# Expert items of 32 slots instead of 64 in a routed streaming step, with four column tiles per product and 8 KB weight runs

## The chip, the cores and the metric

The kernel runs as one program on one core of a Trainium2 chip. The metric is the device time of one execution in microseconds (us); lower is better. The kernel before was executed three times for its time and once more under the hardware profiler, and the changed kernel is measured beside it. The program has five instruction streams: TensorE (PE in the profile; its weight loads are PEld), VectorE (DVE), ScalarE (ACT), GpSimd (POOL) and SyncE (SP), which issues the large transfers.

## The reference, cut to what matters

```python
# N = 384 tokens (256 of a prompt, 8 x 16 of running streams), D = 1024, float32
x = x + mixers(rms_norm(x)) @ w_o                      # first stage, not touched by the change
xn = rms_norm(x, norm2_g)                              # (384, 1024)
lg = xn @ rg_w + rg_b;  p = softmax(lg);  grp = argmax(p)          # 1 group of 4
le = (xn @ re_w + re_b) restricted to grp; the best two of its 8 experts, softmax of the two, times p[grp]
combine = per token two non-zero weights over the 32 experts
for e in range(32):                                    # D_EXPERT = 512
    hdn = silu(xn @ w_gate[e]) * (xn @ w_up[e])        # w_gate, w_up: (1024, 512) each
    out = out + combine[:, e:e+1] * (hdn @ w_down[e])  # w_down: (512, 1024)
y = rms_norm(x + out, final_norm_g)
```

Each of the 384 tokens goes to 2 of 32 experts, 768 pairs in all. For the inputs used, the reference's routing gives the experts 0 to 31 this many tokens: 34 41 7 14 | 8 9 13 6 | 18 20 7 5 | 21 3 7 13 | 32 73 35 37 | 6 12 17 18 | 10 48 18 62 | 28 72 5 69. The bars separate groups of four.

## The kernel before, in words

The first 380 us hold the mixers: 20 chunks of weights are loaded (SP), split into a high and a low part (ACT, POOL) and multiplied (line 1294); convolutions run on DVE. The change does not touch them. From about 403 us on the kernel works off **items**. An item is one expert with up to T = 64 of its tokens ("slots"); an expert with more tokens has more items, and every expert has at least one. There are 35 items. PE, ACT and DVE each run the same loop over them, written as a loop over 16 pairs of experts with the body of `side` 0 and of `side` 1 one after the other, and inside each side a loop over the expert's items. How many items an expert has, and the running numbers, are read from `table` by each engine at the head of each side (`value_load`, four of them on PE: lines 1471 to 1477). In side 1 the first item is written out by itself (line 1482) and the further ones stand in a second body behind a test `n > 1` (line 1483), so that the PE program of a pair holds three item bodies.

One item on PE (function `item`, lines 1427 to 1468) does in this order:

- gate and up (line 1420): the 64 slots as two halves of 32; for each half in use 8 row blocks times 4 column tiles of 128 x 256 weights in float32, results in one PSUM bank, 32 partitions per column tile. The second half runs only if its slots hold tokens (`second_slots`, read from the table);
- for a body that adds back (`c` is not None: side 0 always, side 1 from its second item on), `combine` (line 1413): the collected outputs of the items before, `y_hi` and `y_lo`, are multiplied by a 0/1 matrix `back_to` for three tiles of tokens, and DVE adds the three tiles to `x_tok` (line 1138, `add_rows`);
- gather of the next item's tokens (line 1382): 8 blocks times 3 bfloat16 parts times 3 token tiles, 72 products with the 0/1 matrix `pick`, which DVE builds (lines 1087 and 1091);
- transposes of the hidden rows (line 1452), then down (line 1463): 4 row blocks times 2 column tiles of 128 x 512 weights.

ACT computes silu (line 791), copies the transposed rows (794) and rounds the output to `y_hi` (800); DVE multiplies gate and up and the routing coefficient (1170), scales the gathered tokens (1101), builds `pick`, `back_to` (1181, 1184) and the coefficients (1144, 1149) and forms `y_lo` (1200). The output of an item goes to the half `side` of the partitions of `y_hi` and `y_lo`, so that two experts are collected before rows are added back.

The 192 MiB of expert weights pass through a ring of six slots of 2 MiB, three (gate, up, down) for each of two experts. SP fills them in 1 MiB transfers (line 442), in the order gate, up, gate, up, down, down of each expert; a transfer waits until the expert two before has finished with that half of the slot (`gate_up_half`, `gate_up_done`, `down_half`, `down_done`). The source rows of gate and up are runs of 2 KB, those of down 4 KB.

## Time and profile before

| | before |
|---|---|
| median of 3 runs | 950.26 us (949.14 to 950.53) |
| the profiled execution's own time | 950.75 us |
| its span, first to last instruction | 949.0 us |
| granted TensorE clock, mean over the span | 0.950 |
| PE busy | 834.0 us (88%) |
| DVE busy | 559.4 us (59%) |
| ACT busy | 303.2 us (32%) |
| POOL busy | 270.4 us (28%) |
| bytes moved by DMA | 250.00 MB |
| chain that ended last: PE, DMA | 67%, 20% of the span |

The span is the profiled execution from its first to its last instruction; 1.75 us of the execution's time lie around it. "Busy" counts an engine's instructions; for PE it also counts the time in which products wait in the pipeline, so that a busy PE need not be at its peak. An idle time is put down to what ended it; "issue" means that nothing the profile shows was waited for: the engine's own instruction stream was late.

### The profile page before, as it was taken

What the parts mean: (1) busy time and instruction counts of PE and PEld (TensorE: products, weight loads), DVE (VectorE), ACT (ScalarE), POOL (GpSimd) and SP (SyncE); (2) the same over time, 40 slices, a digit from 0 to 9 for tenths busy, and PEclk for the clock granted to TensorE, in tenths of its full rate; (3) what the DMA queues carried; (4) which work ended last, traced back from release to release, by engine and by line L of the source; (5) the groups of instructions that cost most, each with busy time, mean ns of one, the idle gap of its engine ahead of it and who ended that gap; (6) DMA issues with size and microseconds to landing.
All of it is one profiled execution on the core that took longest, in us unless ns stands there. A gap on an engine that the chain in (4) does not pass through costs nothing.

```text
span 949.0 us, 22550 instructions
## 1 busy us (share of the span) xinstructions
PE 834.0 (88%) x8411; PEld 622.4 (66%) x8412; DVE 559.4 (59%) x1516; ACT 303.2 (32%) x522; POOL 270.4 (28%) x136
## 2 busy tenths in 40 slices
PE   3999999979999999286999777887999988879994
PEld 2999999969999988153555444544565545445562
DVE  3066797899432342844677455545666764646766
ACT  4432875543358332511122111112112221211112
POOL 3745899875767780400000000000000000000000
PEclk9999999989999999598999799979999999999997
DMA  5744244344433323949899999999999999999901
GB/s 210 220 132 134 90 133 134 90 138 134 133 102 120 133 76 125 399 154 377 340 393 396 393 396 392 396 392 397 392 397 392 397 392 397 392 397 392 394 2 66
DMA packets 110200, 250.00 MB, mean 263 GB/s; under 512 B 6282, under 2 KB 6282, under 8 KB 110164
## 3 DMA queue, kind: packets, MB, share of 16 engines
q1 hardware_dynamic: 106528, 244.86, 70.3%
q10 hardware_dynamic: 3636, 4.66, 1.7%
q8 instruction: 22, 0.36, 0.2%
q14 instruction: 14, 0.11, 0.0%
HBM read 246.75 MB, written 2.75 MB: 263 GB/s over the span
## 4 chain that ended last, share of the span: by engine, by line
PE 67%; DMA 20%; DVE 5%; issue 3%; ACT 2%; POOL 1%; ACTq 0%; DVEq 0%; POOLq 0%
PE bank L1294 26%; DMA ring<-in_exp_w_up 19%; PE bank L1420 13%; PE bank L1463 8%; PE bank L1382 6%; PE bank L1413 6%; PE bank L1292 3%; DVE bank L922 2%; DMA stage<-in_norm_g 1%; POOL w_lo L490 1%; PE bank L1452 1%; PE bank L1355 1%; ACT w_hi L610 1%; ACT cvb L683 1%; PE bank L1336 0%
## 5 line engine op out<-in xcount | busy, mean ns | idle before, releaser
L1420 PE MATMUL bank<-ring,cvb 128*32 128x256 f32 x2816 | 178.0, 406 | 60.4 <-DMA ring<-in_exp_w_up 42.4
L490 POOL TENSOR_TENSOR w_lo<-raw,w_hi 128x2048 fp32r<-128x2048 f32 x40 | 184.9, 4623 | 79.8 <-ACT w_hi L610 79.7
L1420 PEld LDWEIGHTS bank<-ring,cvb 128*32 128x32 f32 x2816 | 95.7, 116 | 153.5 <-issue 109.7
L1294 PE MATMUL bank<-x_hi,w_hi 128*128 128x384 f32 x448 | 151.0, 337 | 0.3 <-DVE ua L941 0.2
L1294 PE MATMUL bank<-x_lo,w_hi 128*128 128x384 f32 x448 | 149.9, 335 | 0.0
L1294 PE MATMUL bank<-x_hi,w_lo 128*128 128x384 f32 x448 | 149.9, 335 | 0.0
L922 DVE SCALAR_TENSOR_TENSOR bank<-ub,vec,bank 128x256 f32<-128x256 f32 (+1 forms) x416 | 137.3, 420 | 0.0
L1463 PE MATMUL bank<-ring,cvb 128*64 128x512 f32 x560 | 127.9, 599 | 0.0
L1170 DVE SCALAR_TENSOR_TENSOR cvb<-bank,slot_coef,cvb 64x256 f32<-64x256 f32 x70 | 31.2, 487 | 155.5 <-ACT cvb L791 155.5
L610 ACT ACTIVATE w_hi<-raw 128x2048 fp32r<-128x2048 f32 x40 | 76.6, 1919 | 85.0 <-PE bank L1294 76.6
L800 ACT ACTIVATE y_hi<-bank 64x512 fp32r<-64x512 f32 x70 | 41.4, 591 | 175.8 <-PE bank L1463 175.0
L1138 DVE TENSOR_TENSOR x_tok<-bank,x_tok 128x512 f32<-128x512 f32 x120 | 75.6, 685 | 32.9 <-PE bank L1413 32.5
L1382 PE MATMUL bank<-cvb,ua 128*128 128x64 bf16 x1728 | 85.4, 195 | 0.0
L1294 PEld LDWEIGHTS bank<-x_hi,w_hi 128*128 128x128 f32 x448 | 84.1, 188 | 1.6 <-DVE ua L941 0.5
L1294 PEld LDWEIGHTS bank<-x_lo,w_hi 128*128 128x128 f32 x448 | 84.2, 188 | 0.3
L1294 PEld LDWEIGHTS bank<-x_hi,w_lo 128*128 128x128 f32 x448 | 84.1, 188 | 0.0
L1382 PEld LDWEIGHTS bank<-cvb,ua 128*128 128x128 bf16 x1728 | 69.5, 98 | 21.8 <-issue 15.6
L1463 PEld LDWEIGHTS bank<-ring,cvb 128*64 128x64 f32 x560 | 37.1, 137 | 61.7 <-issue 59.9
L1382 PE MATMUL bank<-cvb,cva 128*128 128x64 bf16 x864 | 72.8, 194 | 0.0
L791 ACT ACTIVATE cvb<-bank 64x256 f32<-64x256 f32 x70 | 22.5, 370 | 154.1 <-PE bank L1420 154.1
L1413 PE MATMUL bank<-y_hi,back_to 128*128 128x512 f32 x120 | 55.6, 463 | 3.7 <-DVE y_lo L1200 3.7
L1200 DVE TENSOR_TENSOR y_lo<-bank,y_hi 64x512 fp32r<-64x512 f32 x70 | 48.2, 688 | 16.3 <-ACT y_hi L800 15.2
(218 smaller groups left out, 1059.6 us busy)
## 6 DMA issues: line engine op xcount, KB each, us to landing
ring<-in_exp_w_gate SPq DMA_DIRECT2D x64, 1024.0 KB, 14.5
ring<-in_exp_w_up SPq DMA_DIRECT2D x64, 1024.0 KB, 14.6
ring<-in_exp_w_down SPq DMA_DIRECT2D x64, 1024.0 KB, 14.0
raw<-in_w_in SPq DMA_DIRECT2D x28, 1024.0 KB, 5.2
raw<-in_w_out_a SPq DMA_DIRECT2D x4, 1024.0 KB, 5.1
raw<-in_w_out_b SPq DMA_DIRECT2D x4, 1024.0 KB, 5.0
raw<-in_w_o SPq DMA_DIRECT2D x4, 1024.0 KB, 5.1
out<-n_tok ACTq DMA_DIRECT2D x3, 512.0 KB, 2.7
```

The source lines that it names most:

```text
L490: pool.tensor_tensor(w_lo[u % NW][:, :, :], raw[u % NW][:, :, :], w_hi[u % NW][:, :, :].bitcast(F32), ALU.subtract).then_inc(lo_ready, 1)
L610: act.activation(w_hi[u % NW][:, :, :], raw[u % NW][:, :, :], ACT.Copy).then_inc(hi_ready, 1)
L800: act.activation(y_hi[side * T:(side + 1) * T, h * HALF:(h + 1) * HALF], Y[h * T:(h + 1) * T, :], ACT.Copy).then_inc(y_hi_ready, 1)
L922: ins = dve.scalar_tensor_tensor(done[part] if tap == KB_TAPS - 1 else acc[part], src, w, done[part] if tap == first else acc[part], ALU.m ...
L1138: last = dve.tensor_tensor(xs, back(t)[h][:, :], xs, ALU.add)
L1170: last = dve.scalar_tensor_tensor(hid[:, cols], gate_and_up(second)[T:2 * T, :], slot_coef[T:2 * T, second:second + 1], sig[:, cols], ALU. ...
L1200: last = dve.tensor_tensor(y_lo[rows, cols], Y[h * T:(h + 1) * T, :], y_hi[rows, cols].bitcast(F32), ALU.subtract)
L1294: ins = pe.matmul(b, wp[:, k % UK, cols], xp[:, k, :], start=start, stop=stop)
L1382: last = pe.matmul(XE[:, k * T:(k + 1) * T], parts[c][:, i, k * P:(k + 1) * P], pick[:, i, :], start=(c == 0 and i == 0), stop=(c == 2 and ...
L1413: last = pe.matmul(b[:, :], back_to[:, t * P:(t + 1) * P], y[:, h * HALF:(h + 1) * HALF], start=(part == 0), stop=(part == 1))
L1420: last = pe.matmul(gate_and_up(second)[q * TQ:(q + 1) * TQ, :], xe[:, k, second * TQ:(second + 1) * TQ], wide(slots[q // 2])[:, k, q % 2 * ...
L1463: last = pe.matmul(Y[h * T:(h + 1) * T, :], hidT[:, k, :], deep(slots[2])[:, k, h * HALF:(h + 1) * HALF], start=(k == 0), stop=(k == HK - 1))
```

## The change

Four things are changed together.

1. T is 32. An expert with more than 32 tokens has two or three items, and there are no halves within an item any more: gate and up are the 32 products that one half had, and the `If` on `second_slots` and its table are gone. Down is four column tiles of 128 x 256 instead of two of 128 x 512, and the output of an item lies in four groups of 32 partitions.
2. `SIDES` = 4: the loop over experts is a loop over eight groups of four with the bodies of sides 0 to 3 one after the other. Rows are added back by side 0 and by the second and third items of the other sides, so once for four experts where each has one item.
3. The weights' rows are assigned to partitions so that a half slot of gate, up or down is one run of 8 KB per partition. The columns of the tokens are permuted to match (`by_row`), with a second copy of the norm's weights (`norm2_by_row`) loaded by one more small transfer on ACT's queue.
4. DVE builds `pick` with two instructions instead of six, and the coefficient of all slots with one instruction over 128 x 768 instead of two over 128 x 384 and two sums.

The core of the diff:

```diff
-    T = 64
-    TQ = T // 2
+    T = 32
+    SIDES = P // T
...
-        w_gu = {0: w_gate.rearrange("l e (k p) c -> (l e) p k c", p=P), 1: w_up.rearrange("l e (k p) c -> (l e) p k c", p=P)}
-        w_dn = w_down.rearrange("l e (k p) c -> (l e) p k c", p=P)
+        w_gu = {0: w_gate.rearrange("l e (h p j) c -> (l e) h p (j c)", h=2, p=P),
+                1: w_up.rearrange("l e (h p j) c -> (l e) h p (j c)", h=2, p=P)}
+        w_dn = w_down.rearrange("l e (h p j) c -> (l e) h p (j c)", h=2, p=P)
+
+        RJ = KB // 2
+
+        def by_row(t):
+
+            return t.rearrange("p (h q j) -> p h j q", h=2, q=P)
 
...
-                    dst, src = (deep(slot), w_dn) if c == 2 else (wide(slot), w_gu[c])
-                    n = (HK if c == 2 else KB) // 2
-                    blocks = slice(h * n, (h + 1) * n)
-                    sp.dma_start(dst[:, blocks, :], src[e, :, blocks, :] if first else
-                                 src[bass.ds(e, 1), :, blocks, :].rearrange("e p k c -> p (e k) c"))\
+                    src = w_dn if c == 2 else w_gu[c]
+                    sp.dma_start(ring[slot][:, h * 2048:(h + 1) * 2048], src[e, h] if first else
+                                 src[bass.ds(e, 1), h, :, :].rearrange("e p x -> p (e x)"))\
...
+            act.dma_start(norm2_by_row[:, :].rearrange("p (h j) -> p h j", h=2),
+                          norm2_g.rearrange("l (h p j) -> p (l h) j", h=2, p=P)).then_inc(rw_in, 16)
...
-                    act.activation(dst[:, i, :], x_tok[:, i, :], ACT.Copy, scale=small[:, 32 + i:33 + i])\
-                       .then_inc(done, 1)
+                    act.activation(dst[:, i, :].rearrange("p (h j q) -> p h j q", h=2, j=RJ), by_row(x_tok[:, i, :]),
+                                   ACT.Copy, scale=small[:, 32 + i:33 + i]).then_inc(done, 1)
...
-                for second in range(2):
-                    act.activation(sig[:, second * QE:(second + 1) * QE], gate_and_up(second)[0:T, :], ACT.Silu)\
-                       .then_inc(sig_ready, 1)
+                act.activation(sig, GU[0:2 * T, :], ACT.Silu).then_inc(sig_ready, 1)
...
-                for h in range(2):
-                    act.activation(y_hi[side * T:(side + 1) * T, h * HALF:(h + 1) * HALF],
-                                   Y[h * T:(h + 1) * T, :], ACT.Copy).then_inc(y_hi_ready, 1)
...
+                for q in range(SIDES):
+                    act.activation(y_hi[side * T:(side + 1) * T, q * QE:(q + 1) * QE],
+                                   Y[q * T:(q + 1) * T, :], ACT.Copy).then_inc(y_hi_ready, 1)
...
-            def pick_tokens(pick_base, pick_n):
-
-                for i in range(NT):
-                    dve.tensor_scalar(pick[:, i, :], iota[:, :], slot_rem[:, 0, i:i + 1], None, ALU.is_equal)\
-                       .then_inc(pick_half, 1)
-                for i in range(NT):
-                    dve.wait_ge(pick_half, pick_base + i + 1)
-                    last = dve.scalar_tensor_tensor(pick[:, i, :], iota[:, :], slot_rem[:, 1, i:i + 1],
-                                                    pick[:, i, :], ALU.is_equal, ALU.add)
-                last.then_inc(picked, 1)
+            def pick_tokens(pick_n):
+
+                dve.tensor_tensor(chosen, iota[:, :].unsqueeze(1).to_broadcast([P, 2 * NT, T]),
+                                  slot_rem.rearrange("p c i -> p (c i)").unsqueeze(2).to_broadcast([P, 2 * NT, T]),
+                                  ALU.is_equal).then_inc(chosen_ready, 1)
+                dve.wait_ge(chosen_ready, pick_n + 1)
...
-            def next_coefficients(n):
-
-                for c in range(2):
-                    dve.scalar_tensor_tensor(at_slot[:, c, :], spread_rows[:, c, :], own_slot[:, 2:3],
-                                             spread_rows[:, 2 + c, :], ALU.is_equal, ALU.mult,
-                                             accum_out=coef_part[:, c:c + 1]).then_inc(coef_half, 1)
-                dve.wait_ge(coef_half, n * 2 + 2)
-                for second, found in enumerate((slice(T, P), slice(0, T))):
-                    dve.tensor_tensor(slot_coef[T:P, second:second + 1], coef_part[found, 0:1],
-                                      coef_part[found, 1:2], ALU.add).then_inc(slot_coef_ready, 1)
...
+                flat = spread_rows.rearrange("p c n -> p (c n)")
+                dve.scalar_tensor_tensor(at_slot.rearrange("p c n -> p (c n)"), flat[:, 0:2 * N],
+                                         own_slot[:, SIDES:SIDES + 1], flat[:, 2 * N:4 * N], ALU.is_equal, ALU.mult,
+                                         accum_out=slot_coef[:, 0:1]).then_inc(slot_coef_ready, 1)
...
-            def gate_up(part, slots, second):
-                for k in range(part * KB // 2, (part + 1) * KB // 2):
-                    for q in range(4):
-                        last = pe.matmul(gate_and_up(second)[q * TQ:(q + 1) * TQ, :],
-                                         xe[:, k, second * TQ:(second + 1) * TQ],
-                                         wide(slots[q // 2])[:, k, q % 2 * QE:(q % 2 + 1) * QE],
-                                         start=(k == 0), stop=(k == KB - 1))
-                return last
-
-            def item(i, slots, filled, c, second_slots):
+            def item(i, slots, filled, c):
 
                 pe.wait_ge(xe_ready, i + 1)
 
                 for part, done in enumerate((gate_up_half, gate_up_done)):
                     pe.wait_ge(weights_in[slots[0]][part], filled)
                     pe.wait_ge(weights_in[slots[1]][part], filled)
-                    with pe.If(second_slots):
-                        gate_up(part, slots, 1)
-                    gate_up(part, slots, 0).then_inc(done, 1)
+                    for k in range(part * KB // 2, (part + 1) * KB // 2):
+                        for q in range(SIDES):
+                            last = pe.matmul(GU[q * T:(q + 1) * T, :], xe[:, k, :],
+                                             wide(slots[q // 2])[:, k, q % 2 * QE:(q % 2 + 1) * QE],
+                                             start=(k == 0), stop=(k == KB - 1))
+                    last.then_inc(done, 1)
...
-                        for h in range(2):
-                            last = pe.matmul(Y[h * T:(h + 1) * T, :], hidT[:, k, :],
-                                             deep(slots[2])[:, k, h * HALF:(h + 1) * HALF],
+                        for q in range(SIDES):
+                            last = pe.matmul(Y[q * T:(q + 1) * T, :], hidT[:, k, :],
+                                             deep(slots[2])[:, k, q * QE:(q + 1) * QE],
...
-            with pe.Fori(0, NE // 2) as pair:
-                for par in range(2):
-                    e = pair * 2 + par
+            with pe.Fori(0, NE // SIDES) as quad:
+                for side in range(SIDES):
+                    e = quad * SIDES + side
                     n = pe.value_load(table[0:1, bass.ds(e, 1)], min_val=1, max_val=N // T)
                     first = pe.value_load(table[0:1, bass.ds(e + NE, 1)], min_val=0, max_val=MAX_ITEMS - 1)
-                    slots = [3 * par + c for c in range(3)]
-                    filled = pair * 16 + 16
+                    slots = [3 * (side % 2) + c for c in range(3)]
+                    filled = quad * (16 * SIDES // 2) + (16 * (side // 2) + 16)
                     back_first = pe.value_load(table[0:1, bass.ds(e + (2 * NE + 1), 1)], min_val=0,
                                                max_val=MAX_ITEMS - 1)
-                    quarters = pe.value_load(table[0:1, bass.ds(e + (3 * NE + 2), 1)], min_val=1, max_val=N // TQ)
-                    if par == 0:
+                    if side == 0:
                         with pe.Fori(0, n) as j:
-                            item(first + j, slots, filled, back_first + j, quarters > j * 2 + 1)
+                            item(first + j, slots, filled, back_first + j)
                     else:
-                        item(first, slots, filled, None, quarters > 1)
+                        item(first, slots, filled, None)
                         with pe.If(n > 1), pe.Fori(1, n) as j:
-                            item(first + j, slots, filled, back_first + j, quarters > j * 2 + 1)
+                            item(first + j, slots, filled, back_first + j)
 
             pe.wait_ge(y_ready, items + 2)
             pe.wait_ge(back_ready, items + 1)

```

The change's item bodies stand one after the other in the program of each engine. Two places on PE show what an item's end and an expert's head consist of; the names are those of the program, and "x16" says that a row stands for 16 instructions of the same form.

PE, end of the first item of the last side of a loop iteration, and the jump over the second body, before:

```order
L1452 MATMUL bank<-ident,cvb 128x64 x4
L1382 MATMUL bank<-cvb,ua 128x64 x6
L1382 MATMUL bank<-cvb,cva 128x64 x3
L1382 MATMUL bank<-cvb,ua 128x64 x6
L1382 MATMUL bank<-cvb,cva 128x64 x3
L1463 MATMUL bank<-ring_54,cvb 64x512 x8
L1483 COMPARE_AND_BRANCH
L1483 UNCONDITIONAL_BRANCH
L1483 ISA
```

Behind the gather of the next item's tokens stands down with 8 of its 16 products in a row, then the test. The same place with the change, at side 1:

```order
L1421 MATMUL bank<-ident,cvb 128x2x32 x2
L1359 MATMUL bank<-cvb,ua 128x32 x6
L1359 MATMUL bank<-cvb,cva 128x32 x3
L1359 MATMUL bank<-cvb,ua 128x32 x6
L1359 MATMUL bank<-cvb,cva 128x32 x3
L1432 MATMUL bank<-ring_54,cvb 32x256 x16
L1451 COMPARE_AND_BRANCH
L1451 UNCONDITIONAL_BRANCH
L1451 ISA
```

The transposes are half as many, the gather's products are as many and half as wide, and down has twice the products at half the width and half the rows. The first row of line 1483 (now 1451) tests `n > 1`, and the second body lies behind it; this structure stands once in the loop before and three times now.

PE, the table reads at the head of side 1, before:

```order
L1471 ISA
L1471 TENSOR_LOAD table
L1471 ISA x2
L1472 ISA
L1472 TENSOR_LOAD table
L1472 ISA x2
L1475 ISA
L1475 TENSOR_LOAD table
L1475 ISA x2
L1477 ISA
L1477 TENSOR_LOAD table
L1477 ISA x2
```

There are four reads, of the number of items, the first item's number, the add-back's number and the halves in use. Now:

```order
L1440 ISA
L1440 TENSOR_LOAD table
L1440 ISA x2
L1441 ISA
L1441 TENSOR_LOAD table
L1441 ISA x2
L1444 ISA
L1444 TENSOR_LOAD table
L1444 ISA x2
```

One of four reads per expert is gone.

## Rows read from the trace of the kernel before

**Rows 1.** The page, part 2: DMA busy share, in tenths, 40 slices.

```profile
DMA  5744244344433323949899999999999999999901
```

**Rows 2.** By line, 380:949 (count, busy us, mean ns, idle); last row: waits.

```profile
L1420 PE MATMUL bank<-ring,cvb 128*32 128x256 f32 x2816 | 178.0, 406 | 60.4 <-DMA ring<-in_exp_w_up 42.4 <-issue 17.4
L1463 PE MATMUL bank<-ring,cvb 128*64 128x512 f32 x560 | 127.9, 599 | 0.0
...
L1138 DVE TENSOR_TENSOR x_tok<-bank,x_tok 128x512 f32<-128x512 f32 x120 | 75.6, 685 | 32.9 <-PE bank L1413 32.5
...
L1413 PE MATMUL bank<-y_hi,back_to 128*128 128x512 f32 x120 | 55.6, 463 | 3.7 <-DVE y_lo L1200 3.7
...
PE bank L1420 <- DMA ring<-in_exp_w_up: 42.4, 19, 3.4
```

**Rows 3.** Stretches: us, busy (count) PE, PEld, DVE, ACT, POOL; PEclk, DMA, GB/s.

```profile
0.00:403.00 403.00, 363.38 (x2075) 350.55 (x2077) 236.71 (x637) 197.31 (x313) 270.37 (x136) 0.96 0.44 147
441.80:448.80 7.00, 0.00 (x0) 0.00 (x0) 1.38 (x2) 2.46 (x3) 0.00 (x0) 0.69 1.05 400
448.80:455.40 6.60, 6.52 (x65) 3.00 (x66) 0.00 (x0) 0.00 (x0) 0.00 (x0) 0.56 0.44 174
475.90:489.00 13.10, 12.93 (x168) 7.67 (x168) 8.68 (x20) 2.74 (x6) 0.00 (x0) 1.00 1.04 396
536.00:543.00 7.00, 7.00 (x95) 4.70 (x95) 4.95 (x11) 0.38 (x1) 0.00 (x0) 0.96 1.05 387
546.60:548.80 2.20, 2.20 (x45) 1.51 (x42) 1.46 (x3) 0.17 (x1) 0.00 (x0) 1.00 1.03 411
```

**Rows 4.** Chain of waits, two items: start us, us, what.

```profile
475.92 3.66 PE bank L1420 x64
479.58 2.04 PE bank L1413 x8
...
482.17 0.39 PE bank L1452 x4
482.56 1.16 PE bank L1382 x36
...
485.26 3.58 PE bank L1463 x16
488.85 0.21 issue
489.06 3.66 PE bank L1420 x64
492.72 1.42 PE bank L1382 x45
...
495.60 3.58 PE bank L1463 x16
499.19 0.83 issue
```

**Rows 5.** The stage's first and last PE rows (chain; timeline: start us, us).

```profile
410.05 8.80 PE bank L1420 x128
...
925.84 3.65 PE L1463 MATMUL bank<-ring,cvb 128*64 128x512 f32 x16
```

**Rows 6.** DMA queues in 0:403, 403:449.5, 449.5:949 (packets, MB, share).

```profile
q8 instruction: 16, 0.26, 0.3%
...
q8 instruction: 6, 0.10, 1.0%
...
q1 hardware_dynamic: 74537, 176.79, 93.7%
q10 hardware_dynamic: 432, 1.57, 0.8%
issues: line engine op xcount, KB each, median us to landing
```

**Rows 7.** Chain of waits at the end of the first loop turn.

```profile
441.80 7.08 issue
448.88 6.48 PE bank L1420 x64
```

**Rows 8.** SP's first transfer in the loop (timeline); the final stores (page, part 6).

```profile
415.62 0.39 SPq L442 DMA_DIRECT2D ring<-in_exp_w_gate  x1
...
out<-n_tok ACTq DMA_DIRECT2D x3, 512.0 KB, 2.7
```

More of the change, by code:

```diff
@@ L180, in trunk_program @@
         vec = sb("vec", [P, KB, NV])
+        norm2_by_row = sb("norm2_by_row", [P, KB])
         ident = sb("ident", [P, P])
@@ L891, in _ @@
             dve.wait_ge(consts, 13)
-            dve.memset(own_slot[T:P, 0:1], -BIG).then_inc(own_slot_ready, 1)
-            dve.memset(own_slot[0:T, 1:2], -BIG).then_inc(own_slot_ready, 1)
-            odd = own_slot[T:P, 1:2]
-            dve.tensor_scalar(odd, odd, -float(T), None, ALU.add).then_inc(own_slot_ready, 1)
-            for g in range(P // TQ):
-                own = own_slot[g * TQ:(g + 1) * TQ, 2:3]
-                first_of = TQ if g < 2 else 0
-                dve.tensor_scalar(own, own, float(first_of - g * TQ), None, ALU.add).then_inc(own_slot_ready, 1)
+            dve.memset(own_slot[:], -BIG).then_inc(own_slot_ready, 1)
+            dve.wait_ge(own_slot_ready, 1)
+            for g in range(SIDES):
+                rows = slice(g * T, (g + 1) * T)
+                for col in (g, SIDES):
+                    dve.tensor_scalar(own_slot[rows, col:col + 1], lane[rows, :], -float(g * T), None, ALU.add)\
+                       .then_inc(own_slot_ready, 1)
             conv_b_at = {}
@@ L1175, in item @@
                     take_gathered(i + 2)
-                    pick_tokens(i * NT + 2 * NT, i + 2)
-                mine = slice(T, 2 * T) if c is None else slice(0, 2 * T)
+                    pick_tokens(i + 2)
+                mine = slice(side * T, (side + 1) * T) if c is None else slice(0, P)
                 own = own_slot[mine, side:side + 1]
@@ L1447, in item @@
                 gather([early])
[L1448 to L1452 removed]
+                turned = HT.rearrange("p (h c t) -> p h c t", h=2, c=HK // 2)
+                cols = hid.rearrange("t (q c) -> t c q", c=HK // 2)
+                for c2 in range(HK // 2):
+                    last = pe.transpose(turned[:, :, c2, :], cols[:, c2, :], ident[0:2 * T, 0:2 * T])
                 last.then_inc(hid_turned, 1)
```

147 lines of the change are left out of this document (63 added, 84 removed).

## The prediction, made before the changed kernel was run

> **What bounds the kernel now.** I read the busy shares by slice first, then the by-line list of the expert stage, then the chain of waits inside it, then the DMA queues. From 449 us on the 16 DMA engines are busy in nearly every slice [rows 1], and PE still waits 42.4 us for weights [rows 2]: the weights set the pace there. One transfer of 1 MiB takes 1.0486 MB / 387 GB/s = 2.71 us in 2 KB runs and 2.55 us in 4 KB runs [rows 3]; the 30 experts loaded inside the loop take 120 x 2.71 + 60 x 2.55 = 478 us. The chain shows that PE is close behind [rows 4]: an item without add-back is 3.66 (gate and up) + 2.88 (gather, transposes) + 3.58 (down) = 10.12 us, one with add-back 3.66 + 5.68 + 3.58 = 12.92. The stage runs from the first gate product at 410.05 to the last down product at 925.84 + 3.65 = 929.49 [rows 5]: 519.4 us. Before it lie 410.05, behind it 19.5, around the span 1.75: 950.75, which is 0.5 above the median of the runs.
>
> **Items.** The line list has 2,816 gate and up products, 64 to a set of 32 slots: 44 sets, and 560 down products, 16 to an item: 35 items [rows 2]. With T = 32 each set is an item: 44. The add-back is named as halved, but 120 of its products at 6 to an add-back are 20 [rows 2], the last one behind the loop; now it runs in every item but the first of sides 1 to 3, 44 - 24 = 20 times in the loop and once behind. It is not reduced at all, and one more lies in the loop than before (19).
>
> **One item on PE.** Gate and up stay 64 products of 128 x 256: 3.66 us. Down becomes 32 products of that same form: half of 3.66, with 0.07 for the mode change 1.90 instead of 3.58. The 72 gather products are half as wide: 36 take 1.16 [rows 4], so they save between 0 (their weight loads stay 128 x 128) and 1.16; I take 0.45, nearer to 0 because the loads don't shrink. Two of four transposes go: 0.39 -> 0.24. Plain item: 10.12 - 1.68 - 0.60 = 7.84. Item with add-back: 12.92 - 2.28 + 0.30 = 10.94; the 0.30 is a wait for y_lo, since down is shorter while DVE must still finish six additions of 0.685 [rows 2], the gathered tokens, pick, back_to and the coefficients. DVE's own savings (two instructions for pick, one for the coefficients) are covered by PE at every other place and count nothing. Sum: 24 x 7.84 + 20 x 10.94 = 407.0.
>
> **Between experts.** From the start of down to the next gate product PE's instruction stream takes 488.85 + 0.21 - 485.26 = 3.80 us from side 0 to 1 and 499.19 + 0.83 - 495.60 = 4.42 around the loop [rows 4]: four table reads, branches, and issue. Down hid 3.58 of it. Now one read of four is gone (a quarter, 0.95), 32 more instructions are issued (0.6 by the pace of a set, 128 in 3.66 us at the slowest), and down hides only 1.90: 1.55 and 2.15 stay bare. 24 x 1.55 + 7 x 2.15 + 12 x 0.2 (second and third items) = 54.7, against 15.8 before. The first item at low clock adds 8.80 - 7.32 = 1.5 [rows 5]. So PE's chain without anything else is 463 us, 56 shorter than the stage now.
>
> **Instruction fetch.** This decides. PE's instructions come over queue q8 in pieces of 16 KB: 16 before 403 us, in which PE issued 2,075 products and 2,077 weight loads, so about 256 to a piece; six more until 449.5; and none in the 500 us after [rows 6, 3]. Each piece was fetched once; the loop of three bodies (2 x 464 + 440 = 1,368 instructions with weight loads, 5.3 pieces) is then kept. Once, at the end of the first turn, PE jumped over a body not yet fetched: 7.08 us without an instruction, where every later turn has 0.83 [rows 7, 4]. So a jump to instructions that aren't there costs 6.25 us. With the change the loop is four bodies of 364 and three of 340, 2,476 instructions, 9.7 pieces, 1.8 times as long. Nothing in the trace shows more than seven pieces held. If the older ones are overwritten, every turn fetches the whole loop again; straight on, that is fetched ahead as in the first 403 us, but a jump over a body (1.4 pieces) lands where nothing is, and so does the jump back. There are 16 jumps over a body (24 experts on sides 1 to 3, less eight with over 32 tokens) and 7 back: 23. Price: 6.25 was seen with DMA at 400 GB/s [rows 3]. Where DMA is idle it is less; the nearest row is the final store at 2.7 us [rows 8]. PE will be the slower side, so DMA will be idle part of the time: 4.4 each, 101.2 us; bounds 62 and 144. Each idle stretch also drops the granted clock: after the one seen it was 0.56, and 64 products took 6.48 instead of 3.66 [rows 3, 7]. 18 such stretches (five jumps follow another at once) x 2.4, somewhat under the 2.8 seen, = 43.2.
>
> The Trainium skill ("Runtime: NRT & Kernel Launch", Instruction fetch mechanics) says that PE's instruction memory holds 2,048 instructions, first in, first out, and that a taken branch out of it waits for a fetch; by it the loop before stays and the new one doesn't. No row shows the 2,048.
>
> **The sum.** 407.0 + 54.7 + 1.5 + 101.2 + 43.2 = 607.6, against 519.4; the shorter routing (the second table's products and copy are gone) starts the stage 1.0 earlier: +87. 950.75 + 87 = 1038, on the median's scale **1037**. The bounds of the fetch give 999 and 1080, those of the gather and the bare stretches about 10 more to each side: 990 to 1085.
>
> **The weight runs.** Halving the number of runs saved 0.16 of 2.71, so halving again saves 0.08: 2.47 us per transfer, 180 x 2.47 = 445, 33 less than now; if the chip splits runs at 4 KB it is 459. In the forecast this is hidden: PE's chain is the longer. The extra small load on ACT's queue and the permuted reads of x_tok lie before 403 us beside other loads; I take 0 and at most 2 us. The Trainium skill ("DMA: Bandwidth & Descriptors", Where 436 GB/s comes from) says that memory at about 358 GB/s per core binds such loads, which speaks against any gain by longer runs. The trace disagrees with 387 and 411.
>
> **Rivals.** (1) *The longer loop is kept after all.* Then weights bind: 445 us instead of 478, and the gain is real. Against it count that the first slot is now released by expert 0's second item, at about 424 instead of the 415.62 at which SP issues now [rows 8], and that in the groups with 8 items PE needs 3 x 7.84 + 5 x 10.94 + 8 = 86 us where weights need 59. By slice (23.7 us each) DMA is full from the 18th, with one gap in it, to the end of the 38th [rows 1]: some 498 us for the 478 of transfers, 20 idle, most of it before 415.62; I estimate 35 to 50 now, and 3 more behind the last weights. 445 + 35 to 50 + 3 - 498: -15 to 0, with the cheapest gather and bare stretches -20: **942** (930 to 953). For it: the loop before shows no refetch at all. It decides from about seven pieces held to ten. (2) *Only the farthest are lost*: the pieces at the end and the start overwrite each other, the middle stays. Then 5 jumps on side 3 and 7 back miss: 463 + 12 x 4.4 + 7 x 2.4 = 533, +13, and some waits for weights: **970**. (3) The engines' chain around y_lo and add-back costs more than 0.3 per item, 1 us or so: +14 on either case; no row speaks for it: in an item with add-back DVE is busy 8.68 of 13.1 us [rows 3].
>
> **Chances.** Forecast 0.58; rival 1 0.25, of which 0.20 faster by over 0.2% (about what a measurement can tell) and 0.05 within it; rival 2 0.12; slower in another way 0.05. Faster 0.20, same 0.05, slower 0.75. The range leaves out the fast end of rival 1 and the slow end of the forecast: 938 to 1075; the likeliest case alone is 990 to 1085.
>
> **What would show it.** Queue q8 with well over 28 pieces, spread over the whole stage (about 10 per turn); PE idle 5 to 8 us with "issue" at 18 places, between experts 1|2, 2|3, 3|4 of a group; low clock behind each; GB/s by slice below 380; 44 items of 7.8 and 10.9 us; down at 1.9. Wrong: q8 at about 27 with none after the first turn; then rival 1. A plain item above 8.5 us would break the item sum.

## The result, and the profile after

The changed kernel takes 1062.37 us (median of 4 runs, 1060.63 to 1065.03) against 950.39 for the kernel before in the same runs: a ratio of 1.118, 95% interval 1.115 to 1.121. It is 112 us slower. The forecast was 1037, in a range of 938 to 1075.

| | before | after |
|---|---|---|
| profiled execution, its span | 950.75, 949.0 us | 1061.03, 1059.3 us |
| stage of experts, first gate product to the end of the last down product | 410.05 to 929.5: 519.4 us | 407.90 to 1039.3: 631.4 us |
| PE busy in the stage | 461.6 us | 442.7 us |
| granted clock in the stage | 0.95 | 0.86 |
| pieces of instructions on queue q8 | 22 | 111 |

The page of the profile after, parts 2 and 3: granted clock, DMA share and rate in 40 slices of 26.5 us, and the queue of PE's instructions (packets, MB, share).

```profile
PEclk9999999899999968987887768779998769889997
DMA  6633333434432292896996988964788967955601
GB/s 220 203 120 120 120 120 120 125 125 135 139 112 88 67 369 91 330 419 278 419 395 271 414 327 338 387 269 204 295 347 338 416 278 306 410 243 240 239 2 59
...
q8 instruction: 111, 1.82, 0.7%
```

Ahead of the experts little moved: the stage starts at 407.90 us instead of 410.05, 2.1 earlier where 1.0 was forecast. From the 17th slice on DMA, full in [rows 1], has holes, and the clock has dips that the kernel before did not have. Queue q8 moves 111 pieces: 16 of them before 403 us as in [rows 6], and 95 behind. These are the lines that answer to [rows 2] (count, busy us, mean ns, idle before them):

```profile
L1402 PE MATMUL bank<-ring,cvb 128*32 128x256 f32 x2816 | 198.4, 444 | 186.5 <-issue 186.5
...
L1432 PE MATMUL bank<-ring,cvb 128*32 128x256 f32 x1408 | 85.1, 382 | 0.0
...
L1389 PE MATMUL bank<-y_hi,back_to 128*128 128x512 f32 x126 | 54.6, 433 | 8.2 <-DVE y_lo L1180 8.2
```

Gate and up still have 2,816 products, but the idle time before them is 186.5 us, all "issue": the engine's stream was late. The 42.4 us of waiting for weights are gone. Down has 1,408 products, 32 to each of 44 items. The add-back has 126 of its products of this form, 6 more than before (20 in the loop and one behind it). What PE waited for (us in total, times, longest):

```profile
PE bank L1402 <- issue: 186.5, 32, 15.0
PE bank L1389 <- DVE y_lo L1180: 8.2, 5, 4.5
```

The 32 times are one ahead of the stage (1.50) and one for each of the 31 places between experts. They fall into three kinds: 13 of 1.29 to 1.46 us, 12 of 6.95 to 8.04 with one of 4.50, and five of 14.37 to 15.00. One turn shows all three, here the chain of waits of PE from the first products of expert 4 to those of expert 6, and the stop behind expert 7 (start us, us, what; left out are the rest of expert 4's item and all between expert 6's first products and that stop), which answers to [rows 4]:

```profile
492.10 5.37 PE bank L1402 x64
...
504.67 1.45 issue
506.12 3.66 PE bank L1402 x64
509.78 1.47 PE bank L1359 x54
511.25 0.38 PE bank L1421 x2
511.63 0.55 PE bank L1359 x18
512.17 1.86 PE bank L1432 x32
514.04 7.46 issue
521.49 6.03 PE bank L1402 x64
...
548.95 14.37 issue
```

Expert 4, on side 0, ends with 1.45 us of head: the part of the next expert's table reads and branches that down does not cover. There is no more, since side 1's first body lies right behind side 0's in the program. The item of expert 5 takes 3.66 + 1.47 + 0.38 + 0.55 + 1.86 = 7.92 (one with add-back, at full clock, 10.86); then PE jumps over the unused second body of side 1: 7.46. The next such jump took 6.95, and where the jump over side 3's second body is followed by the jump back, 14.37. Behind each, the 64 products take some 5.3 to 6.5 us instead of 3.66. The stretches, with columns as in [rows 3]:

```profile
407.90:1039.30 631.40, 442.71 (x7720) 294.88 (x7720) 309.62 (x729) 104.87 (x269) 0.00 (x0) 0.86 0.74 301
477.20:492.00 14.80, 0.00 (x0) 0.00 (x0) 1.86 (x5) 2.75 (x5) 0.00 (x0) 0.66 0.79 320
514.10:521.40 7.30, 0.00 (x0) 0.00 (x0) 1.87 (x6) 1.50 (x4) 0.00 (x0) 0.64 1.02 424
521.50:527.40 5.90, 5.90 (x64) 3.06 (x64) 0.00 (x0) 0.00 (x0) 0.00 (x0) 0.59 1.02 418
1002.90:1007.40 4.50, 0.00 (x1) 0.03 (x1) 1.95 (x6) 1.50 (x4) 0.00 (x0) 1.00 0.02 4
```

The first is the whole stage. The second holds two jumps in a row (14.8 us without a product), the third one jump, at 424 GB/s; the fourth is the gate and up behind it, at a clock of 0.59: most of it at the lower of the two levels, 1.2 GHz. In the fifth, the only jump after the last weights had arrived (at about 1001), the DMA engines are empty, and it took 4.50.

### The profile page after: what moved, and what is told of

Read it like the earlier page. It is cut to its first block, busy times and chain, and to the rows that moved or that the text cites. A ratio compares the mean times of both kernels' runs of the same rounds, so it can differ in the third digit from the quotient of the medians.

```text
span 1059.3 us, 25276 instructions
## 1 busy us (share of the span) xinstructions
PE 814.0 (77%) x9866; PEld 650.6 (61%) x9867; DVE 559.3 (53%) x1388; ACT 317.5 (30%) x604; POOL 270.3 (26%) x136
## 4 chain that ended last, share of the span: by engine, by line
PE 69%; issue 19%; DVE 6%; ACT 2%; POOL 1%; DMA 1%; ACTq 0%; DVEq 0%; POOLq 0%
PE bank L1274 23%; PE bank L1402 17%; PE bank L1359 8%; PE bank L1432 7%; PE bank L1389 6%; PE bank L1272 3%; DVE bank L922 2%; PE bank L1421 2%; DMA stage<-in_norm_g 1%; POOL w_lo L491 1%; DVE y_lo L1180 1%; PE bank L1335 1%; ACT w_hi L611 1%; ACT cvb L684 0%; PE bank L1316 0%
## 5 line engine op out<-in xcount | busy, mean ns | idle before, releaser
L1402 PE MATMUL bank<-ring,cvb 128*32 128x256 f32 x2816 | 198.4, 444 | 186.5 <-issue 186.5
L1402 PEld LDWEIGHTS bank<-ring,cvb 128*32 128x32 f32 x2816 | 112.5, 127 | 270.3 <-issue 236.6
L1151 DVE SCALAR_TENSOR_TENSOR cvb<-bank,slot_coef,cvb 64x256 f32<-64x256 f32 x44 | 21.5, 489 | 273.1 <-ACT cvb L793 273.0
L801 ACT ACTIVATE y_hi<-bank 32x256 fp32r<-32x256 f32 x176 | 66.0, 375 | 137.9 <-PE bank L1432 134.7
L793 ACT ACTIVATE cvb<-bank 64x256 f32<-64x256 f32 x44 | 16.6, 376 | 292.7 <-PE bank L1402 292.7
L1127 DVE TENSOR_TENSOR x_tok<-bank,x_tok 128x512 f32<-128x512 f32 x126 | 79.3, 684 | 33.8 <-PE bank L1389 31.7
L1359 PEld LDWEIGHTS bank<-cvb,ua 128*128 128x128 bf16 x2160 | 79.0, 96 | 24.2 <-issue 21.2
L1359 PE MATMUL bank<-cvb,ua 128*128 128x32 bf16 x2160 | 91.6, 177 | 0.0
L1432 PE MATMUL bank<-ring,cvb 128*32 128x256 f32 x1408 | 85.1, 382 | 0.0
L1359 PE MATMUL bank<-cvb,cva 128*128 128x32 bf16 x1080 | 81.2, 176 | 0.0
L1180 DVE TENSOR_TENSOR y_lo<-bank,y_hi 32x256 fp32r<-32x256 f32 x176 | 74.0, 420 | 6.4 <-ACT y_hi L801 4.3
L1432 PEld LDWEIGHTS bank<-ring,cvb 128*32 128x32 f32 x1408 | 41.3, 109 | 24.0
```

The source lines that it names most:

```text
L801: act.activation(y_hi[side * T:(side + 1) * T, q * QE:(q + 1) * QE], Y[q * T:(q + 1) * T, :], ACT.Copy).then_inc(y_hi_ready, 1)
L1127: last = dve.tensor_tensor(xs, back(t)[h][:, :], xs, ALU.add)
L1180: last = dve.tensor_tensor(y_lo[rows, cols], Y[q * T:(q + 1) * T, :], y_hi[rows, cols].bitcast(F32), ALU.subtract)
L1359: last = pe.matmul(XE[:, k * T:(k + 1) * T], parts[c][:, i, k * P:(k + 1) * P], pick[:, i, :], start=(c == 0 and i == 0), stop=(c == 2 and ...
L1402: last = pe.matmul(GU[q * T:(q + 1) * T, :], xe[:, k, :], wide(slots[q // 2])[:, k, q % 2 * QE:(q % 2 + 1) * QE], start=(k == 0), stop=(k ...
L1432: last = pe.matmul(Y[q * T:(q + 1) * T, :], hidT[:, k, :], deep(slots[2])[:, k, q * QE:(q + 1) * QE], start=(k == 0), stop=(k == HK - 1))
```

## The experiments

Theory A is the prediction's: PE's loop over experts has become too long to be kept, so that every turn is fetched again, and a jump whose target is not there costs a fetch. The experiments first take the length away and leave the rest, then add length and nothing else.

### E1: the change, with PE's loop folded

```diff
-            with pe.Fori(0, NE // SIDES) as quad:
-                for side in range(SIDES):
-                    e = quad * SIDES + side
+            with pe.Fori(0, NE // SIDES) as quad, pe.Fori(0, 2) as late:
+                for par in range(2):
+                    e = quad * SIDES + late * 2 + par
...
-                    if side == 0:
-                        with pe.Fori(0, n) as j:
-                            item(first + j, slots, filled, back_first + j)
-                    else:
-                        item(first, slots, filled, None)
-                        with pe.If(n > 1), pe.Fori(1, n) as j:
-                            item(first + j, slots, filled, back_first + j)
+                    start = late if par == 0 else 1
+                    if par == 0:
+                        with pe.If(late > 0):
+                            item(first, slots, filled, None)
+                    else:
+                        item(first, slots, filled, None)
+                    with pe.If(n > start), pe.Fori(start, n) as j:
+                        item(first + j, slots, filled, back_first + j)
```

> The changed kernel with PE's loop over experts folded: two item positions (even and odd expert of a pair) serve all four sides, so that the loop is four bodies, some 1,410 instructions instead of 2,476; the items, their order, the add-backs and everything on the other engines are the change's. Theory A (PE's loop is too long to be kept, every turn is fetched again): queue q8 moves 22 to 25 pieces instead of 111, no PE idle stretch with 'issue' over 2 us after the first turns, weights bind again, 942 us (930 to 953). Rival B (the 7 to 15 us stretches belong to the jumps over a body and back in this four-sided program, whatever the loop's length: table reads, branches, late semaphores): the jumps are all still there, one more per pair even, so at least 1040. Rival C (part of the added time lies in the items of 32 themselves): between the two, plain items over 8 us.

Measured: 957.64 us (955.93 to 959.11), ratio to before 1.008 (1.006 to 1.010), and 23 pieces on q8. PE's waits (us, times, longest):

```profile
PE bank L1402 <- issue: 44.7, 23, 3.0
PE bank L1402 <- DMA ring<-in_exp_w_up: 43.8, 21, 3.8
```

No wait over 3.0 us, where theory A had said 2, and the weights bind again in places. Rival B falls, and 105 of the change's 112 us are gone with PE's loop alone folded. But 957.6 is not the 942 (930 to 953) that the prediction and theory A gave to a kept loop, and the change without its fetches is still 7 us slower than the kernel before. E3 to E5, E10 and E11 look for that.

### E2: the kernel before, with PE's loop written out twice

```diff
-            with pe.Fori(0, NE // 2) as pair:
-                for par in range(2):
-                    e = pair * 2 + par
+            with pe.Fori(0, NE // 4) as quad:
+                for side in range(4):
+                    par = side % 2
+                    e = quad * 4 + side
...
-                    filled = pair * 16 + 16
+                    filled = quad * 32 + (side // 2 * 16 + 16)
```

> The kernel before, with nothing changed but PE's loop over pairs of experts written out twice per turn (8 turns of four experts, six bodies of 464 and 440, 2,736 instructions instead of 1,368). Same items of 64, same jumps over a body (13), same waits. Theory A: every turn is fetched again; 13 jumps over a body and 7 back miss, 6 us each by the changed kernel's rows (7.4 less the 1.4 of a hit) = 120, 13 stretches drop the clock, 2.3 each = 30; against that the 42 us of waiting for weights go: 950 + 150 - 42 = 1058 (1030 to 1085), q8 over 80 pieces, 7 stretches near 14 us, 6 near 7. Rival B: 950, q8 near 22 pieces, no stretch over 2 us.

Measured: 1061.38 us (1059.63 to 1062.10), ratio 1.116 (1.115 to 1.118), q8 119 pieces. No item, no product and no transfer differs from the kernel before, and the time is 111 us above it. That it equals the changed kernel's is chance: here 20 jumps miss, there 23, and the items are others. The chain of waits of PE (start us, us, what) shows a jump over a body, a bare head, and a jump over a body with the jump back:

```profile
592.65 8.56 issue
...
616.21 0.43 issue
...
628.10 14.31 issue
```

There are six of the first kind at 8.6 to 8.7 and seven of the last at 14.1 to 14.3. The counts are those expected and so are the double ones, but the single ones were put near 7; why one takes 8.6 here, more than the change's 7.4, though down hides more of the head, was not found. Six waits of 1.3 to 1.5 us for "issue" ahead of the gather (L1382, 7.4 us in all), which the kernel before does not have, come on top.

### E3: the kernel before, with 8 KB runs alone

```diff
-                    dst, src = (deep(slot), w_dn) if c == 2 else (wide(slot), w_gu[c])
-                    n = (HK if c == 2 else KB) // 2
-                    blocks = slice(h * n, (h + 1) * n)
-                    sp.dma_start(dst[:, blocks, :], src[e, :, blocks, :] if first else
-                                 src[bass.ds(e, 1), :, blocks, :].rearrange("e p k c -> p (e k) c"))\
+                    src = w_dn if c == 2 else w_gu[c]
+                    sp.dma_start(ring[slot][:, h * 2048:(h + 1) * 2048], src[e, h] if first else
+                                 src[bass.ds(e, 1), h, :, :].rearrange("e p x -> p (e x)"))\
```

with `by_row` on the tokens, `norm2_by_row`, and the transposes reading every second column, as in the change.

> The kernel before with the change's third part alone: rows of the weights in runs of 8 KB, tokens' columns permuted to match. In the changed kernel's full slices DMA moves 417 to 426 GB/s, so 2.49 us per transfer against 2.71 and 2.55: 180 x 2.49 = 448, 30 less than 478, and the 42 us in which PE waits for weights are there to take it: 920 us (912 to 930). If longer runs are worth nothing while PE also reads the weights, or the permuted reads cost: 950.

Measured: 926.72 us (925.56 to 930.42), ratio 0.976 (0.974 to 0.979): 24 us faster than the kernel before, and the fastest of all that were run with all their work. Its waits, which halve the 42.4 of [rows 2]:

```profile
PE bank L1429 <- DMA ring<-in_exp_w_up: 20.0, 11, 2.9
PE bank L1429 <- issue: 19.9, 22, 6.7
```

### E4: E1 with the old runs

The same lines as in E3, turned back in E1.

> E1 with the weights' rows in the old runs of 2 and 4 KB. Theory A with weights binding: transfers take 478 us as before, with 35 to 50 us in which the queue is empty because slots are released later: 968 (960 to 985), 25 to 30 above E1. If PE's chain of items binds in E1 and not the weights: within 8 us of E1.

Measured: 979.01 us (978.95 to 979.65), ratio 1.030 (1.029 to 1.032), 21.4 above E1. The runs are worth 21 to 24 us with items of either size. Of E4 and then E1, a stretch in which the queue is full in both:

```profile
520.00:690.00 170.00, 116.64 (x1918) 71.86 (x1922) 70.68 (x172) 27.49 (x69) 0.00 (x0) 0.84 1.04 394
```

```profile
403.00:423.00 20.00, 17.87 (x269) 11.30 (x265) 10.57 (x26) 6.55 (x13) 0.00 (x0) 0.88 0.03 6
520.00:640.00 120.00, 85.29 (x1387) 52.30 (x1384) 50.80 (x125) 19.76 (x50) 0.00 (x0) 0.83 1.01 422
700.00:728.00 28.00, 26.53 (x515) 18.61 (x512) 20.12 (x48) 6.55 (x19) 0.00 (x0) 1.00 0.60 238
878.00:884.00 6.00, 5.98 (x115) 3.53 (x114) 5.41 (x14) 1.50 (x4) 0.00 (x0) 1.00 0.11 19
```

The second row of E1 has 422 GB/s against 394: 1.0486 MB takes 2.48 us. Its other rows are taken up below.

### E5: two sides instead of four

```diff
-            with pe.Fori(0, NE // SIDES) as quad:
-                for side in range(SIDES):
-                    e = quad * SIDES + side
+            with pe.Fori(0, NE // 2) as pair:
+                for side in range(2):
+                    e = pair * 2 + side
```

the same on ACT and DVE, with the table of add-backs and `filled` to match.

> The changed kernel with its second part undone: items of 32 slots, 8 KB runs, but the loops of all engines run over pairs of experts (sides 0 and 1), so that rows are added back by side 0 and by further items: 28 add-backs in the loop instead of 20. PE's loop is three bodies, some 1,070 instructions plus heads. Theory A (length of the loop alone made the change slow): q8 22 to 24 pieces, no stretch over 3 us; against E1 (957.6) PE has 8 add-backs more (10.86 - 7.92 = 2.9 each, 23 in all), of which only those count where PE and not the weights are late, and heads without E1's extra branch (0.5 to 0.6 less at half of them): 950 to 965, 957. If the four sides as such cost something that E1 still has: under 945. If the add-backs count in full: 975 or more.

Measured: 960.78 us (959.29 to 963.35), ratio 1.011 (1.009 to 1.013), q8 21 pieces. Three bodies instead of seven, nothing else for PE to fetch, and no wait over 1.9 us for its stream:

```profile
PE bank L1402 <- DMA ring<-in_exp_w_up: 43.2, 21, 3.8
PE bank L1402 <- issue: 38.2, 24, 1.9
```

That is 3 us above E1, about as much as either's runs spread. E5 adds rows back eight times more and E1 has the fold's extra branch and loop, so what adding back less often is worth by itself was not separated. Items of 32, four column tiles and the lighter DVE work together cost 34 us against E3, which has the same runs.

### E6 to E8: instructions that are never executed

E3 with a branch at the end of PE's loop that is never taken, of 120, 250 and 380 products (240, 500 and 760 instructions with their loads):

```diff
+                        with pe.If(n > N // T - 1):
+                            for _ in range(250):
+                                pe.matmul(XE[:, 0:T], parts[0][:, 0, 0:P], pick[:, 0, :], start=True, stop=True)
```

> E3 (the kernel before with 8 KB runs, 926.7 us, q8 22 pieces) with a third, never executed branch at the end of PE's loop over pairs, 120 small products long (240 instructions with their loads): the loop spans 1,690 instructions, 6.6 pieces, executed work unchanged. Theory A gives no count; it says that somewhere between 5.7 pieces (E3, kept) and 9.7 (the change, lost) the loop stops being kept, and that the time then jumps at once, by 16 returns of the loop that miss. Here: q8 23 or 24, 927 to 930. The Trainium skill (Runtime: NRT & Kernel Launch, Instruction fetch mechanics) gives 2,048 instructions, first in, first out: by it this loop is kept. Rival B (long stretches come from jumps over bodies, not from length): the same time.

> As E6 with 250 products (500 instructions) in the branch: the loop spans 1,950 instructions, 7.6 pieces, and touches eight of them, with the piece that is fetched ahead nine. By the change's rows (each turn lost costs the pieces again, about 6 us at a jump that misses, 2.3 at low clock) it is 927 if kept; if lost, 15 returns and up to 13 jumps over the second body miss: 1000 or more, q8 over 80. By the Trainium skill's 2,048 instructions (Runtime: NRT & Kernel Launch, Instruction fetch mechanics) the loop itself would still fit, though not with the piece ahead. I expect it lost, 0.6.

> As E6 with 380 products (760 instructions) in the branch: the loop spans 2,210 instructions, 8.6 pieces. Theory A: lost, q8 over 100 pieces, 1000 to 1060 us. Rival B, by which only executed instructions or jumps over bodies matter: 927 to 932, q8 at 24.

Measured, one run each: 933.02, 1190.95 and 1184.56 us, with 23, 159 and 159 pieces on q8. E6, with a loop of 6.6 pieces, keeps it (us, times, longest; its one wait of 12.7 stands in the first turn, where E3 has one of 6.7, and those 6 us are what it lies above E3 and most of why it lies above the 927 to 930 expected):

```profile
PE bank L1429 <- issue: 28.4, 21, 12.7
PE bank L1429 <- DMA ring<-in_exp_w_up: 20.8, 11, 3.0
```

E7, 260 instructions longer and with the same work, loses it. The chain of waits of PE in one of its turns:

```profile
533.64 18.74 issue
...
567.31 0.26 issue
...
577.93 19.24 issue
```

Three jumps in a row (over the second body, over the branch, back) cost 18.4 to 19.5 us, 6.2 each. The forecast of E8, 1000 to 1060, was far too low: almost every turn misses three jumps, and PE waits 278.6 us for "issue" in E8 and 280.6 in E7. In E8 the branch is 1.5 times as long as in E7 and nothing more is lost: what counts is whether the loop is kept and how many jumps there are, not how far they go. The pieces are counted here with heads, waits and branches, 1,450 instructions or 5.7 pieces for the kernel before; the prediction's 5.3 are products and weight loads alone. The Trainium skill (Runtime: NRT & Kernel Launch, Instruction fetch mechanics) has 2,048 instructions in PE's memory, first in, first out, with the next block fetched ahead. E7's loop of 1,950 is under that and was lost; by its length it touches at least eight blocks and needs a ninth for the piece ahead, so that the runs agree with the Trainium skill if the piece ahead is counted. No run shows that piece by itself. The same section of the Trainium skill says that a jump out of the current two blocks waits. The kernel before, E1 and E6 jump back over 5.7 to 6.6 pieces with stops of 0.8 to 2.9 us and 22 or 23 pieces on q8 in the whole program, so that half of it does not hold here.

### E9: the change with little traffic

```diff
-                    sp.dma_start(ring[slot][:, h * 2048:(h + 1) * 2048], src[e, h] if first else
-                                 src[bass.ds(e, 1), h, :, :].rearrange("e p x -> p (e x)"))\
+                    sp.dma_start(ring[slot][:, h * 2048:(h + 1) * 2048] if first else
+                                 ring[slot][:, h * 2048:h * 2048 + 128], src[e, h] if first else
+                                 src[bass.ds(e, 1), h, :, 0:128].rearrange("e p x -> p (e x)"))\
```

> The changed kernel, but the 180 transfers of weights inside the loop bring only the first 512 bytes of each 8 KB run (64 KB instead of 1 MB): the experts from the third on are computed with what lies in the ring, PE's loop and its jumps are the change's. It measures what a missed jump costs when the DMA engines have nothing else to do. In the changed kernel a single one shows 7.4 us (1.4 of them without a miss) at 418 to 425 GB/s, a double one 14.6 at 310 to 320, so 6.0 to 6.6 each, where the prediction took 4.4 by supposing idle DMA. Theory P (a missed jump waits mostly on traffic): under 5.8 us and under 11 us, 23 x 2 = 46 us less in all, 1015. Rival Q (the fetch costs the same without traffic): 7.0 to 7.5 and 14 to 15, 1055 to 1062.

Measured, one run: 1003.40 us, 59 less than the change, with the same 111 pieces. The chain of waits over the first two such places, and the stretch of the second:

```profile
459.03 4.67 issue
463.70 6.14 PE bank L1403 x64
...
474.12 9.86 issue
483.98 6.24 PE bank L1403 x64
```

```profile
474.20:483.90 9.70, 0.00 (x0) 0.00 (x0) 1.88 (x6) 2.76 (x5) 0.00 (x0) 0.75 0.08 19
```

A single missed jump takes 4.35 to 5.49 us, a double one 9.58 to 9.86, where the change has 7.4 and 14.6. Taking off 1.4 for the head, a miss costs 3.7 on average without traffic (129.9 us of "issue", less 1.5 ahead of the stage and 31 x 1.4, over 23) and 6.2 with it. Between these two the price does not simply follow the traffic: the change's single misses cost 6.0 at a DMA share of about 1.0, its double ones 6.6 each at 0.75 to 0.79, and E7's 6.2 each at 0.46 to 0.62 (five of its stops). Only the step from an almost empty queue to a used one is shown. Theory P holds, and by more than was expected of it. The low clock behind each place is there as before (6.14, 6.24 for 64 products).

### E10 and E11: E1 and E3 with little traffic

The edit of E9 in E1 and in E3.

> E1 (items of 32, folded loop) with only 64 KB in each of the 180 transfers in the loop: the experts from the third on are computed with what lies in the ring, and PE never waits for weights. It shows PE's own chain for 44 items. From rows of the changed kernel and of E1: 24 x 7.92 + 20 x 10.86 = 407, 8 of waits for y_lo, 45 to 50 between experts, a few us at low clock: stage 465, so 408.5 + 465 + 20 + 2 = 896 us. Theory S (items of 32 are no longer for PE in all, but the experts with over 32 tokens hold their ring slots longer, and that starves the queue there): E10 is 5 to 15 below E11 though E1 is 31 above E3. Rival R (items of 32 with their heads simply make PE's chain longer): E10 is 20 to 35 above E11.

> E3 (the kernel before with 8 KB runs) with only 64 KB in each of the 180 transfers in the loop: PE's own chain for 35 items of 64. The stage before took 519.4 us with 42.4 of waits for weights: 477, so 410 + 477 + 20 + 2 = 909 us; 904 to 912, since the one missed jump costs less without traffic. Theory S and rival R as in E10.

Measured, one run each: 919.78 and 902.70 us. The middle of both, first E10 (columns as in [rows 3]):

```profile
413.00:881.00 468.00, 404.15 (x7393) 277.55 (x7386) 296.57 (x699) 101.15 (x261) 0.00 (x0) 0.96 0.09 25
```

```profile
413.00:881.00 468.00, 449.40 (x6256) 266.00 (x6248) 307.24 (x839) 96.37 (x189) 0.00 (x0) 0.99 0.09 25
```

So PE's own chain is 17 us longer with items of 32 in the folded loop, neither shorter (theory S) nor the whole of the 31 us between E1 and E3, nor the 20 that rival R asked for at least. E10 lies 24 us above its forecast of 896, E11 6 below its 909. Over the whole stage PE is busy 424.3 us of 489.2 in E10 and 450.6 of 469.2 in E11, 26 less; but its idle time for "issue" ahead of gate and up is 63.5 us in E10 and 20.5 in E11 (some 2.5 of each ahead of the stage), 43 more. A head that down hid for 3.58 us is hidden for 1.86 now, and shows between experts. Some of these heads lower the clock. Four of E10's, of the two lengths that it has between pairs (chain of waits: start us, us, what):

```profile
563.73 2.91 issue
566.64 5.28 PE bank L1403 x64
...
588.49 2.13 issue
590.62 3.66 PE bank L1403 x64
...
720.84 2.11 issue
722.95 5.35 PE bank L1403 x64
...
810.51 2.86 issue
813.37 3.66 PE bank L1403 x64
```

Of seven heads of 2.86 to 2.95 us six are followed by 64 products at 5.2 to 6.6 us and one by 64 at 3.66; of eight of 2.08 to 2.13 us three are followed by 5.35 and five by 3.66. The longer ones lower the clock more often, but the length of the stop alone does not decide it. Heads of 2.1 to 2.9 us belong to the fold, which adds a branch and a loop; E5 without it has none over 1.9, so part of the 17 is the fold's.

The other 14 us (31 less 17) are there only with the full traffic: weights and items get into each other's way. In the rows of E1 shown under E4, the DMA share is 0.03 from 403 to 423 us, 0.60 from 700 to 728 and 0.11 from 878 to 884. The same stretches of E3, the first two:

```profile
403.00:423.00 20.00, 16.50 (x239) 11.22 (x236) 6.43 (x21) 5.02 (x13) 0.00 (x0) 0.87 0.29 99
700.00:728.00 28.00, 26.99 (x396) 16.14 (x392) 17.50 (x49) 5.71 (x11) 0.00 (x0) 1.00 1.01 416
```

That is 5 us of empty queue more at the start, where expert 0 has two items of 32 and its slots come free with the second, and 11 more in the group of experts 16 to 19 (32, 73, 35 and 37 tokens: eight items instead of five). By the program a slot is held for all items of its expert; that six slots do not bridge four such experts in a row is read from these stretches, no run tries it with more slots.

## Why the prediction was right, and where it was not

**The decision was right.** PE's loop was the point: the count of pieces (about 10 per turn forecast, 95 behind 403 us in eight turns, so about 12), the places (18 stretches, five of them double, 23 missed jumps), the cause "issue", and the low clock behind each are all in the trace. E1 takes the length out, leaves all work as it is and gets 105 us back; E2 puts it into the kernel before and loses 111; E7 does it with instructions that never run.

**The sum, term by term.** The stage was put at 607.6 us and took 631.4:

| term | forecast | measured | from |
|---|---|---|---|
| 44 items at full clock | 407.0 | 405.1 + 3.7 of waits for y_lo | 442.7 busy less 37.6 |
| 31 heads without a miss | 54.7 | 43.4 | 31 x 1.40, the mean of the 13 bare ones |
| 23 missed jumps | 101.2 | 141.6 | 186.5 - 1.5 - 43.4 |
| low clock | 43.2 + 1.5 | 37.6 | 18 x 2.09 over 3.66 |
| sum | 607.6 | 631.4 | |

The items were right to 0.1 us each (7.92 and 10.86 against 7.84 and 10.94); the 0.07 for a mode change in down had no row behind it, and down took 1.86 with or without such a cost. The heads were put at 1.55 and took 1.40 where they can be seen alone; the return of the loop, put at 2.15, missed each time, so that the split between heads and misses rests on 1.40 for all.

**The step that was mis-sized** is "PE will be the slower side, so DMA will be idle part of the time: 4.4 each". A miss cost 6.16 (141.6 / 23), hardly less than the 6.25 of [rows 7] that the prediction had as its upper bound. DMA was indeed idle for part of the stage (share 0.74), but little at the jumps: at 514 us it moves 424 GB/s and from 477 us 320; the expert's gate and up and then its down have just given their slots back. With an empty queue a miss costs less than the 4.4 that were taken: 3.1 in the change's one jump behind the last weights (4.50 less 1.40 of head), 3.7 on average in E9. So 4.4 lay between the two cases, and the case that held was the dear one. This term is 40 us too low; heads and low clock are 18 too high together.

**Rival 1 had the wrong sign.** It gave 942 (930 to 953) to a kept loop. E1 is that case, at 957.6, and E5 at 960.8: slower than before by about 1%. Its transfers were right (2.48 us against 2.47; 180 of them are 447 us). From 403 us to the last weights, at 899.3, E1 takes 496 us, so the queue lacks work for 49 us in all, the far end of the 35 to 50 that were put down: the three rows of E1 from 403, 700 and 878 us give 19.4 + 11.2 + 5.3 = 36 of it, and the rest lies in shorter stretches. And the end was too short: from the last weights to the last down E1 takes 34.7 us and the kernel before 27.6, not 3 but 7 more, since expert 31 has three items of 32. With these figures its own sum gives 447 + 49 + 7 - 498 = +5 in place of -8, which is what E1's profiled run shows (955.93 against 950.75). The 8 KB runs' gain of 24 us (E3) is given back by items of 32, before any fetch.

**Rivals 2 and 3.** No middle of the loop was kept: jumps on all of sides 1 to 3 miss. The wait for y_lo, feared in each item, is 3.7 us in the whole stage (8.2 less the 4.5 behind the loop), in four places where two items with add-back follow each other.

**What stays open.** E5 against E3 bundles the size of the items with part 4 of the change (DVE's fewer instructions), which was not tried alone. Between 6.6 and 7.6 pieces the limit was not searched further. Of E8's being 6 us below E7, one run of each says nothing.

## What to carry to other kernels

Count the instructions of a loop, weight loads included and branches that are never taken too, before unrolling it: at 6.6 pieces of 256 this one ran free, at 7.6 it cost 258 us with the same work, and the profile says so in one line, the count on the instruction queue against the length of the program. Price a missed jump from stops with the traffic that it will meet, not from an idle queue: the empty queue's 3.7 us and the loaded one's 6.2 are 57 us apart over 23 misses. And a shorter item does not shorten the chain where the work hid a head: what is taken from the item comes back bare, and experts with many items hold their buffers longer than the mean shows.

## What the runs showed of the hardware that was not expected

- A jump to instructions that are not there costs 3.7 us on average with an almost empty DMA queue (E9) and 6.2 in the change, where the queue moves 306 to 425 GB/s at all stops but the last.
- Missed jumps in a row add up (7.4 and 14.6 us for one and two in the change, some 18.9 for three in E7, whose down hides more of the head), and passing over 760 instructions instead of 500 (E8, E7) costs no more.
- Rows of 8 KB move at 422 GB/s, 4 KB at 411, 2 KB at 387 (E1, [rows 3]).
- In E10 PE's clock fell behind six of seven stops of 2.9 us and behind three of eight of 2.1; the next 64 products then took 5.2 to 6.6 us instead of 3.66.
